# Gathering decode rows in row groups, and two more places for expert weights beside the ring

## What is computed

```python
lg = hf @ w_group                                   # 4 groups
g = jnp.argmax(lg, axis=-1)
le = (hf @ w_router).reshape(-1, N_GROUPS, EXPERTS_PER_GROUP)
sel = jnp.take_along_axis(le, g[:, None, None], axis=1)[:, 0]
topv, topi = lax.top_k(jax.nn.softmax(sel, axis=-1), 2)   # 2 of 8 experts
gu = jnp.einsum('td,edf->tef', hs, w_gate_up)       # 32 experts, 1024 -> 2 x 256
act = jax.nn.silu(gu[..., :256]) * gu[..., 256:] * gate[..., None]
out = jnp.einsum('tef,efd->td', act, w_down)        # 256 -> 1024
```

## Time and profile before

| | us |
|---|---|
| median of 3 runs | 1205.48 (1205.21 to 1206.83) |
| the profiled execution | 1206.16 |
| its span, first to last instruction | 1204.4 |
| PE busy | 1160.5 (96%) |
| VectorE, ScalarE busy | 359.1, 155.5 |
| mean granted TensorE clock | 0.989 of full |
| DMA | 364.6 MB, 303 GB/s over the span |

### The profile page before, as it was taken

One profiled execution on the slowest core, in us unless ns is written; L12 is line 12 of the kernel. 1 busy time (PEld: TensorE's weight loads), 2 busy tenths in 40 slices (PEclk: granted clock), 3 DMA queues, 4 the chain that ended last, 5 costly groups with the idle time before them and its releaser, 6 DMA issues.

```text
span 1204.4 us, 13793 instructions
## 1 busy us (share of the span) xinstructions
PE 1160.5 (96%) x5930; PEld 684.6 (57%) x5930; DVE 359.1 (30%) x876; ACT 155.5 (13%) x364; POOL 11.8 (1%) x22
## 2 busy tenths in 40 slices
PE   8999999999999999989999999999999999998885
PEld 7567777777554343436655656466677753443333
DVE  5221223212213141445234242423410022342225
ACT  2000002112111110120201011011200021110002
POOL 0000000000000000000000000000000000000000
PEclk9999999999999999999999999999999989999988
DMA  9963336934989999999345656392997469999993
GB/s 370 428 225 140 140 129 281 380 127 155 404 349 375 428 428 427 429 426 417 124 177 224 248 192 279 141 365 97 413 424 317 151 227 374 429 427 428 427 427 163
DMA packets 29744, 364.60 MB, mean 303 GB/s; under 512 B 3456, under 2 KB 3600, under 8 KB 7024
## 3 DMA queue, kind: packets, MB, share of 16 engines
q1 hardware_dynamic: 26784, 339.87, 69.1%
q10 hardware_dynamic: 1712, 19.17, 3.8%
q0 software_dynamic: 1184, 4.63, 1.0%
HBM read 339.34 MB, written 24.32 MB: 302 GB/s over the span
## 4 chain that ended last, share of the span: by engine, by line
PE 86%; DMA 11%; DVE 1%; issue 1%; ACT 0%; SPq 0%; DVEq 0%
PE bank L866 23%; PE bank L568 13%; DMA ring<-in_gu 9%; PE bank L679 7%; PE bank L654 6%; PE bank L950 5%; PE bank L457 5%; PE bank L722 4%; PE bank L451 4%; PE bank L691 3%; DMA ring<-in_vc 2%; PE bank L921 1%; PE bank L1031 1%; PE bank L1012 1%; PE bank L716 1%; PE bank L516 1%
## 5 line engine op out<-in xcount | busy, mean ns | idle before, releaser
L866 PE MATMUL bank<-hT,ring 128*128 128x288 f32 x1088 | 268.2, 407 | 0.9 <-issue 0.9
L866 PEld LDWEIGHTS bank<-hT,ring 128*128 128x128 f32 x1088 | 205.7, 190 | 66.9 <-issue 12.0
L568 PE MATMUL bank<-arena,ring 128*128 128x288 f32 x592 | 146.3, 406 | 0.0
L568 PEld LDWEIGHTS bank<-arena,ring 128*128 128x128 f32 x592 | 111.2, 190 | 29.6
L679 PE MATMUL bank<-ring,arena 128*32 128x512 f32 x896 | 106.5, 618 | 13.8 <-DMA ring<-in_gu 13.7
L654 PE MATMUL bank<-arena 128*128 128x512 f32 (+1 forms) x192 | 97.2, 632 | 0.0
L679 PEld LDWEIGHTS bank<-ring,arena 128*32 128x32 f32 x896 | 28.8, 112 | 84.1 <-issue 73.2
L722 PE MATMUL bank<-arena 128*128 128x288 f32 x256 | 68.9, 413 | 3.1 <-issue 2.8
L654 PEld LDWEIGHTS bank<-arena 128*128 128x128 f32 (+1 forms) x192 | 31.9, 191 | 65.1 <-issue 64.2
L1517 DVE TENSOR_TENSOR xT<-xT,bank 128x288 f32<-128x288 f32 x128 | 58.2, 454 | 32.3 <-PE bank L722 28.6
L722 PEld LDWEIGHTS bank<-arena 128*128 128x128 f32 x256 | 46.2, 190 | 24.5 <-issue 8.4
(11 more groups left out here) (259 smaller groups left out, 899.7 us busy)
## 6 DMA issues: line engine op xcount, KB each, us to landing
ring<-in_gu SPq DMA_DIRECT2D x56, 2048.0 KB, 19.1
ring<-in_dn SPq DMA_DIRECT2D x29, 2048.0 KB, 16.6
...
```

What stands on the lines that cost most here:

```text
L568: mm = pe.matmul(bank[1 + o % 4][:, 0:T], w[k], cat[:, k, :], start=(k == 0), stop=(k == kt - 1))
L866: mm = pe.matmul(outs[o], w[:, o, k, :], src[:, k, :], start=(k == 0), stop=(k == KD - 1))
```

## The change

1. **Gather.** The decode rows of `htok` now lie in four row groups of 32 partitions with a quarter of the 1024 columns each (`htok3`, 256 columns). `picked_decode` makes four products of 32 rows, one per row group, each into its own bank (0, 1, 5, 6) and 256 columns wide; `picked_prompt` adds the two blocks of prompt rows, four times 256 columns. Copies go by quarters, ScalarE 0 and 2, VectorE 1 and 3. Since banks 5 and 6 hold down products, `pick` waits from the third pack on for their copies.
2. **Turned together.** `turn_scaled` turns only the two prompt blocks; the decode rows of four eighths are turned at once by four narrow products at k = 6 and at k = 7 (`decode_rows`).
3. **Sums and ranks.** The choice matrix and sums for decode tokens are repeated in the four row groups, so `token_sums` and the ranks have more, smaller products, and VectorE numbers the third block in two steps of its own.
4. **Banks.** Layer 1's memory products use banks 4 and 3 in turn and not 7. The gate turns (bank 7) then need not wait for their copies; the activation turns (bank 3) do.
5. **Loads.** dn(0,2,0) gets a place outside the ring (number 11), which gu(0,1,2) held before, and is issued ahead of gu(0,3,0). The first half of gu(1,2,0) is loaded into room that the smaller `htok` leaves, and into the constants' waves, ahead of gu(1,0,0); the ring slot then gets only the second half. gu(1,0,3) moves a piece.

```diff
-         ("dn", (1, 2, 1)): 8, ("gu", (1, 3, 0)): 9, ("dn", (0, 2, 1)): 10}
+         ("dn", (1, 2, 1)): 8, ("gu", (1, 3, 0)): 9, ("dn", (0, 2, 1)): 10,
+         ("dn", (0, 2, 0)): 11}
...
-                   ("gu", (0, 3, 0)): (("dn", (0, 2, 1)),),
+                   ("gu", (0, 3, 0)): (("dn", (0, 2, 1)), ("dn", (0, 2, 0))),
...
-               ("dn", (0, 2, 1)): ("gu", (0, 1, 1))}
+               ("dn", (0, 2, 1)): ("gu", (0, 1, 1)), ("dn", (0, 2, 0)): ("gu", (0, 1, 2))}
+SPLIT = ("gu", (1, 2, 0))
...
+                    11: (hT_[:, 0:half], ar(VO, half))}[EXTRA[name]]
+
+        def first_half():
+
+            waves = CC["cos"][0]
+            return ar(PHO + ROUTE + 2304, 1536), cst[:, waves + 1088:waves + 1600]
...
+        KV_BANKS = ((0, 1, 2, 3, 4, 5, 6, 7), (3, 4, 4, 3, 4, 3, 4, 3))
...
+        X_BANKS = (0, 1, 5, 6)
...
+            def load_first_half():
+
+                sp.wait_ge(S("dec_pv"), 8)
+                sp.wait_ge(S("pv_sum"), 8)
+                sp.wait_ge(S("roped"), H)
+                sp.wait_ge(S("r_st"), H)
+                src, o = source(SPLIT), 0
+                for part in first_half():
+                    sp.dma_start(part, src[:, o:o + part.shape[1]]).then_inc(S("half_home"), 16)
+                    o += part.shape[1]
...
+                if name == ("gu", (1, 0, 0)):
+                    load_first_half()
...
+                elif name == SPLIT:
+                    sp.dma_start(slot(n % R)[:, half:SLOT], src[:, half:SLOT]).then_inc(S(f"landed{n % R}"), 16)
...
-                for b, (t0, n) in enumerate(BLK):
-                    mm = pe.transpose(bank[5 + 2 * (k % 2)][0:n, b * P:(b + 1) * P], hT[:, k, t0:t0 + n], C("ident"))
+                for b in range(2):
+                    mm = pe.transpose(bank[5 + 2 * (k % 2)][:, b * P:(b + 1) * P], hT[:, k, b * P:(b + 1) * P],
+                                      C("ident"))
+                if k < KD - 2:
+                    mm.then_inc(S("h_turned"), 1)
+                else:
+                    decode_rows(k % 2)
+
+            def decode_rows(half):
+
+                for g in range(4):
+                    mm = pe.matmul(bank[5 + 2 * half][32 * g:32 * g + 32, 2 * P:3 * P], hT[:, 2 * g + half, TP:T],
+                                   C("ident"), start=True, stop=True, skip_group_check=True)
                 mm.then_inc(S("h_turned"), 1)
...
-                pe.matmul(bank[5][:, 2 * NE:3 * NE], C("ones"), M[:, 1, :], start=False, stop=True,
+                pe.matmul(ranks[:, 2, :], C("ones"), M[:, 1, :], start=False, stop=False, skip_group_check=True)
+                for g in range(4):
+                    pe.matmul(ranks[32 * g:32 * g + 32, 2, :], C("tri", TD)[:, 0:TD], M[0:TD, 2, :], start=False,
+                              stop=True, skip_group_check=True)
+                pe.matmul(ranks[:, 3, :], C("fold", TD), M[0:TD, 2, :], start=False, stop=True,
                           skip_group_check=True).then_inc(S("ranks"), 1)
...
-            def picked(sel, n):
-
-                for b, (t0, m) in enumerate(BLK):
-                    mm = pe.matmul(bank[n][:, :], sel[0:m, b, :], htok[b][0:m, n * 512:(n + 1) * 512],
-                                   start=(b == 0), stop=(b == 2))
+            def picked_decode():
+
+                for m in range(4):
+                    r = slice(32 * m, 32 * m + 32)
+                    pe.matmul(bank[X_BANKS[m]][:, 0:256], onehot_m[r, 2, :], htok3[r, :], start=True, stop=False,
+                              skip_group_check=True)
+
+            def picked_prompt(m):
+
+                for b in range(2):
+                    mm = pe.matmul(bank[X_BANKS[m]][:, 0:256], onehot_m[:, b, :], htok[b][:, m * 256:(m + 1) * 256],
+                                   start=False, stop=(b == 1), skip_group_check=True)
                 return mm
...
                 def pick(i):
                     pe.wait_ge(S("selected"), PACKS * L + i + 1)
-                    for n in range(2):
-                        picked(onehot_m, n).then_inc(S("x_picked"), 1)
+                    if i >= 2:
+                        pe.wait_ge(S("y_out_a"), PACKS * L + i - 1)
+                        pe.wait_ge(S("y_out_d"), PACKS * L + i - 1)
+                    picked_decode()
+                    for m in range(4):
+                        picked_prompt(m).then_inc(S("x_picked"), 1)
...
                         memory_kv(1, j)
-                        pe.wait_ge(S("gt_out"), i)
                         memory_kv(1, j + 1)
-                        pe.wait_ge(S("kv1_out"), j + 2)
...
                     turn_gates().then_inc(S("gt_turned"), 1)
+                    if L == 0 and i in MEMORY_IN:
+                        pe.wait_ge(S("kv1_out"), 2 * MEMORY_IN[i] + 2)
...
-                V_(dve.scalar_tensor_tensor(out=rk, in0=v3(bank[5][:, 0:96], 3), scalar=1.0, in1=M,
+                ranks = v3(bank[5][:, 0:4 * NE], 4)
+                dve.scalar_tensor_tensor(out=rk[:, 0:2, :], in0=ranks[:, 0:2, :], scalar=1.0, in1=M[:, 0:2, :],
+                                         op0=ALU.add, op1=ALU.mult)
+                V_(dve.tensor_copy(M[:, 2, :], ranks[:, 3, :]))
+                V_(dve.scalar_tensor_tensor(out=rk[:, 2, :], in0=ranks[:, 2, :], scalar=1.0, in1=M[:, 2, :],
                                             op0=ALU.add, op1=ALU.mult))
```

131 lines of the change are left out of this document (69 added, 62 removed).

## The result

The changed kernel takes **1194.53 us** (median of 6 runs, 1192.49 to 1198.73); the kernel before, on the same chip, 1206.05 us (6 runs, 1204.76 to 1206.83). The ratio is 0.9911, 95% interval 0.9895 to 0.9926: faster by 10.7 us by the ratio, 11.5 by the medians. Forecast: 1195.4.

A forecast was written before the change was run, and what follows sets the result against it. Both expert stages were taken to end on the DMA stream, PE bounding everything between. 9.3 - 1.7 + 2.5 = 10.1 us off the profiled 1206.16 gives 1196.1; with the median 0.68 lower, 1195.4 us, range 1192.2 to 1200.5.

The forecast's parts named there:

- The gather: Each pack's gather on PE, 16 times: 4.29 us instead of 5.93, 1.64 us less per pack.
- The stream of layer 0: Layer 0's expert loads: earlier issues and a removed 7.4 us stop bring its last gate wait 9.3 us forward.
- the new stop near 424: Layer 0's load stream, before the issue moved from 431.4 to 422.7: a new stop of about 1 us.
- Rival 2: Layer 0's stream: the 7.4 us stop only moves to a later issue; 1201.8 us, chance 0.06.
- Rival 3: Gather: the row groups run one after the other, saving only 0.4 us each; 1202.7 us, chance 0.07.
- Rival 5: Whole kernel: the change does nothing that counts, loads beside the ring land no earlier; 1205 us, chance 0.02.
- rival 4: Layer 0's tail into the retention: the clock falls and stays low, making it slower; 1208.7 us, chance 0.03.
- Banks: Layer 0's packs 1, 3, 5: gate turns move into PE's wait for the second memory copy, 0.5 us each.
- The clock's 1.7 us in layer 0: Layer 0's last pack: longer waits for gate chunks lower PE's clock, so 1.7 us is subtracted.
- Rival 1: Ends of both layers' experts: the clock falls for longer, 6.8 rather than 3.4 us; 1198.8 us, chance 0.20.
- only one such fall in four: Argument against longer clock falls: only pack 5 of layer 1 showed one of 6.8 us.
- Layer 1, 2.5 us forecast: Layer 1's expert stream gains 2.5 us, 0.7 from the half chunk, though the first gather starts 0.9 us late.

The follow-up runs named there:

- experiment 1: Changed kernel with dn(0,2,0) put back into the ring, so without its place outside; 1199.59 us, ratio 0.9945 to the kernel before.
- experiment 2: Kernel before with only the place outside the ring for dn(0,2,0) added; 1205.46 us, ratio 0.9993 to the kernel before.
- experiment 7: Changed kernel with four spare 128x256 multiplications (1.9 us) ahead of each of layer 0's gathers; 1208.83 us, ratio 1.0014 to the kernel before.
- experiment 10: Changed kernel with four spare 128x256 multiplications ahead of layer 0's first five gathers only; 1211.01 us, ratio 1.0042 to the kernel before.
- experiment 6: Changed kernel with the wait for kv1_out back in front of the gate turns in layer 0's three memory packs; 1195.42 us, ratio 0.9908.
- experiment 5: Changed kernel with four spare 128x384 multiplications ahead of the third gate chunk in layer 1's last four packs; 1195.10 us, ratio 0.9905.
- experiment 8: Changed kernel with gu(1,2,0) loaded whole into its ring place and VectorE's two copies of gathered rows moved earlier; 1195.62 us, ratio 0.9905.
- experiment 11: Changed kernel with VectorE's copies of gathered rows moved earlier and spare multiplications in layer 1's waits; 1194.91 us, ratio 0.9900.

## Why the prediction was right

**The gather** was forecast at 4.29 us and takes 4.30. The two rows that it was built from (1.07 for four row groups, 0.219 per pass) carried over.

**The stream of layer 0** was the largest term, 9.3 us with the start of its experts. Measured: 0.7 + 8.5 = 9.2. All five issues are within 0.5 us of the forecast, the first within 0.25; the new stop near 424 is 0.4 us and not 1. Inside the sum two errors cancel, which is luck: the first gather starts 1.0 us late and not 0.4, and from the first gate chunk to the issue near 367 PE gains 4.35 us where the terms give 3.8. That the term is right for its own reason is shown by experiments 1, 2, 7 and 10: take the place away and 5.1 us come back (4.1 by the ratios), take the gather's gain away and 5.7 to 6.0 us of stops come back, the place alone gives nothing clear of the noise. Rival 2 (the stop moves) is what happens on the kernel before, and does not happen with the shorter gathers. Rivals 3 and 5 fell with the first rows, and rival 4 too: no profile has a low clock of more than 10.2 us at a stretch.

**Banks, 0.5 us three times:** 0.61 each by experiment 6, of the 0.69 that PE waited there.

**The clock's 1.7 us in layer 0.** The waits are 1.89 and 3.02 as forecast. The fall did not come in the profiled execution; it came right behind the start of gu(0,7,2), or on it, in those of experiments 1, 5 and 6, and from that start to the retention it is 22.8 us there instead of 21.1: that is the 1.7. In four others it began at 505 to 507 us, around the wait for gu(0,7,1). With 3.4 us it lay in the waits and the stretch stays at 21.1; with 6.8 us (experiment 8) it is 22.4, with 10.2 us (experiment 11) 24.0. So the term is a chance and not a sum, and 1.7 is its price where a fall of 3.4 us comes last. Rival 1's value (1198.8) is close to five of the eleven runs, but no profile of those five was kept, and other profiles have falls at the two routers and behind the last transfer too, so they need not be one mechanism. What the prediction said against it, "only one such fall in four", was a misreading: of the four falls before the last one of the kernel before, two last 6.8 us, at layer 1's router and in pack 5.

**Layer 1, 2.5 us forecast, 3.8 by columns D and E**, and part of the surplus is luck with the clock. The first gather starts 110.5 us behind project_out before and now, where 0.9 late was forecast. The step holds where the clock is alike: in the profiles of experiments 5, 6 and 11 the clock fell 105.1 to 105.5 us behind the start of project_out, in the kernel before 105.3 behind it, and stayed low up to the gather in all four; there the gather starts at 111.4, 0.9 late as forecast. In the changed kernel's own two profiles the fall was 3.4 us long or did not come, and the gather starts at 110.5 and 109.9. What failed is that the sum took the low clock of before as given. The next step gave less than forecast: from gather to gate chunk it is 7.0 us and was 8.1, so 1.1 less instead of 1.8, because the rows wait 1.35 us for VectorE's copies, which stand behind the gate values. I had written that the copies "end at least as early". Together the gate chunk is 1.1 us earlier in this profile, where 0.9 was forecast, 1.7 earlier without a fall, and 0.2 to 0.4 later than before in the three with 10.2 us of low clock. The issue that ends the stop comes 3.0 us earlier, counted from project_out, and the last bulk transfer ends 3.0 earlier too (302.6 us behind it, 305.6 before): the forecast of 2.5 for the stream was 0.5 short. Within it the half chunk was taken at 0.7 and is about 1.0. The other 0.8 us of the 3.8 is in the stretch behind the last bulk transfer (21.2 us before, 20.3 after), which I had not looked at; its cause is open.

So the forecast of the profile, 1196.1, stands 2.0 us above the measured 1194.1: 1.7 for the fall that did not come and 1.3 more in layer 1, less the 0.8 us by which that execution began later. That the median of the runs is within 0.9 us of the forecast is so in part luck: the scatter between two executions of this kernel is larger than each of these three. The upper end of the range was added up wrongly: rival 1's 1198.8 and a gather 1.5 late instead of 0.9 give 1199.4, not 1200.5; nothing measured hangs on it.
